# Engines report ahead of the score units, second keys on GpSimd, embedding projection in three bank pairs

## The reference

```python
def nsa_mixer(u, ...):                       # layer 1, 16 heads of 64 in 4 key groups
    q, kv, gates = split(u @ w_in)           # three branches: compressed, selected, window
    o = g0*softmax(q @ ck)@cv + g1*softmax(rope(q) @ ks)@vs + g2*softmax(rope(q) @ kw)@vw
    return o @ w_o

def channel_and_ple(h, p_i, g_pre, g_post, w_ff_in, w_ff_out, w_pg, w_pp):
    u = rmsnorm(h, g_pre)
    f = square(relu(u @ w_ff_in)) @ w_ff_out
    h = h + rmsnorm(f, g_post)
    return h + sigmoid(h @ w_pg) * (p_i @ w_pp)     # gate product, embedding projection
```

## Time and profile before

| | |
|---|---|
| median of 3 runs | 1681.08 us |
| the profiled execution's own time | 1680.83 us |
| its span, first to last instruction | 1677.9 us |
| busy: TensorE, weight load, VectorE, ScalarE, GpSimd | 1616.1, 1480.2, 824.3, 647.9, 109.2 us |
| granted TensorE clock, mean over the span | 0.987 |
| idle of TensorE ahead of L389 that ends with ACT L838 | 5.5 us in 6 waits |

### The profile page before, as it was taken

One profiled execution on the slowest core, in us unless ns is written; L12 is line 12 of the kernel. 1 busy time (PEld: TensorE's weight loads), 2 busy tenths in 40 slices (PEclk: granted clock), 3 DMA queues, 4 the chain that ended last, 5 costly groups with the idle time before them and its releaser, 6 DMA issues.

```text
span 1677.9 us, 32224 instructions
## 1 busy us (share of the span) xinstructions
PE 1616.1 (96%) x13788; PEld 1480.2 (88%) x13788; DVE 824.3 (49%) x1099; ACT 647.9 (39%) x1141; POOL 109.2 (7%) x138
## 2 busy tenths in 40 slices
PE   8999899999999999999999889999999999999998
PEld 7787799999999998999999555556999999999988
DVE  6988547444342436632342565652464433334462
ACT  5444654232231324522232456664442322323242
POOL 1000000000000000000240332210000000000000
PEclk9999999999999999999999879999999999999999
DMA  7533162323222222231246100002222222222211
GB/s 207 155 100 104 35 207 76 101 76 98 79 81 96 76 101 76 76 103 56 76 145 206 58 1 1 1 14 76 77 85 91 87 91 85 92 84 93 88 64 54
DMA packets 139623, 145.69 MB, mean 87 GB/s; under 512 B 6562, under 2 KB 131314, under 8 KB 139279
## 3 DMA queue, kind: packets, MB, share of 16 engines
q1 hardware_dynamic: 138207, 136.94, 25.9%
q0 software_dynamic: 1280, 6.75, 1.3%
HBM read 130.79 MB, written 10.87 MB: 84 GB/s over the span
## 4 chain that ended last, share of the span: by engine, by line
PE 87%; DVE 7%; ACT 4%; issue 1%; DMA 0%; SPq 0%; DVEq 0%; ACTq 0%
PE ps L389 63%; PE ps L522 2%; PE ps L1207 2%; PE ps L1056 2%; PE ps L1055 2%; PE ps L1057 2%; PE ps L1724 2%; PE ps L1704 1%; PE ps L1706 1%; DVE w_lo L374 1%; PE ps L1651 1%; PE ps L575 1%; PE ps L1649 1%; ACT w_hi L369 1%; DVE neg_max L1838 1%
## 5 line engine op out<-in xcount | busy, mean ns | idle before, releaser
L389 PE MATMUL ps<-x_hi,w_hi 128*128 128x272 f32 x1664 | 361.9, 291 | 15.0 <-ACT ple_proj L838 4.3
L389 PE MATMUL ps<-x_hi,w_lo 128*128 128x272 f32 x1664 | 358.2, 289 | 0.0
L389 PE MATMUL ps<-x_lo,w_hi 128*128 128x272 f32 x1664 | 357.5, 289 | 0.0
L374 DVE TENSOR_TENSOR w_lo<-w_raw,w_hi 128x2048 fp32r<-128x2048 f32 x101 | 233.8, 2315 | 141.4 <-ACT w_hi L369 139.5
L369 ACT ACTIVATE w_hi<-w_raw 128x2048 fp32r<-128x2048 f32 x101 | 192.6, 1907 | 267.9 <-PE ps L389 265.0
L389 PEld LDWEIGHTS ps<-x_hi,w_hi 128*128 128x128 f32 x1664 | 267.4, 189 | 24.5 <-issue 11.5
L389 PE MATMUL ps<-hid_hi,w_hi 128*128 128x272 f32 x1280 | 268.1, 289 | 2.2 <-DVE hid_lo L2028 1.5
L389 PEld LDWEIGHTS ps<-x_lo,w_hi 128*128 128x128 f32 x1664 | 267.9, 190 | 0.0
L389 PE MATMUL ps<-hid_hi,w_lo 128*128 128x272 f32 x1280 | 267.4, 288 | 0.0
L389 PE MATMUL ps<-hid_lo,w_hi 128*128 128x272 f32 x1280 | 266.6, 288 | 0.0
L389 PEld LDWEIGHTS ps<-x_hi,w_lo 128*128 128x128 f32 x1664 | 266.2, 189 | 0.0
(11 more groups left out here) (379 smaller groups left out, 2124.1 us busy)
## 6 DMA issues: line engine op xcount, KB each, us to landing
w_raw<-in_ffn_w_in SPq DMA_DIRECT2D x64, 512.0 KB, 4.5
w_raw<-in_ffn_w_out SPq DMA_DIRECT2D x64, 512.0 KB, 4.2
w_raw<-in_nsa_w_in SPq DMA_DIRECT2D x20, 512.0 KB, 4.5
w_raw<-in_ple_w_gate SPq DMA_DIRECT2D x16, 512.0 KB, 4.2
w_raw<-in_conv_w_in SPq DMA_DIRECT2D x15, 512.0 KB, 5.7
w_raw<-in_conv_w_out SPq DMA_DIRECT2D x8, 512.0 KB, 3.9
w_raw<-in_nsa_w_o SPq DMA_DIRECT2D x8, 512.0 KB, 4.4
conv_in_turned<-conv_in SPq DMA_DIRECT2D x16, 203.2 KB, 2.6
```

Source lines behind the costliest of these rows:

```text
L374: dve.tensor_tensor(WL[par][:, :], RAW[par][:, :], WH[par][:, :].bitcast(F32), ALU.subtract)\
L389: m = pe.matmul(o_, w[par][:, wcols:wcols + P], x[:, k, c_], start=f, stop=l)
```

## The change

It has three parts. (1) The embedding projection uses bank pairs 0, 1 and 3 in the order 0, 1, 3, 0, 1, 3, 0, 3; the copies of blocks 2, then 3 and 4 move ahead in ScalarE's list; the gate product's first slab waits for seven copies, not eight. (2) The three reports of `leave_phase` move into the sample part, ahead of the last early score units (TensorE: one, VectorE: three, ScalarE: two). The eight sample copies move from the end of the sample part to between lead units 5 and 6. Both shifts of the first pair and their rows stand ahead of the compressed branch of group 0 on VectorE; on TensorE the first shift stands behind unit 5 instead of unit 4, the second behind unit 7; `cmp_exp(0)` moves behind unit 8 on ScalarE. (3) GpSimd makes the third query set and the keys of group 1 right behind the second query set, ahead of the compressed blocks; a query set reports each half.

```diff
+        PLE_BLK = (0, 1, 3, 0, 1, 3, 0, 3)
+        PLE_FREE = (-1, 0, None, 1, 2, 3, 4, 6)
...
             for mb in range(NC):
-                pe_block(pe, s % 2, mb % 2, b + mb, s, mb, PH, PL, None, 0, nk=2, width=D)
+                if PLE_FREE[mb] is not None:
+                    pe.wait_ge(blk_free, b + PLE_FREE[mb])
+                pe_block(pe, s % 2, PLE_BLK[mb], b + mb, s, mb, PH, PL, None, 0, nk=2, width=D, free=False)
...
-            pe_slab_by_chunk(pe, s, b, XH, XL, x_ready, 8 * nx)
+            pe_slab_by_chunk(pe, s, b, XH, XL, x_ready, 8 * nx, free=1)
...
             ple(1)
+            ple(2)
             for c in range(NC):
-                if c + 2 < NC:
-                    ple(c + 2)
                 act.wait_ge(S["r_ready"], 8 * nr + c + 1)
                 L(act.activation(XH[:, c, :], R[:, c, :], ACT.Copy), S["xh_ready"], wait=False)
+                if c == 0:
+                    ple(3)
+                if c < 4:
+                    ple(c + 4)
...
             turn(3)
+            leave_phase(pe)
             unit(3)
...
             out_t(3)
+            leave_phase(act)
             unit(2)
             unit(3)
...
             turned(3)
+            leave_phase(dve)
             unit(1)
             unit(2)
             unit(3)
+
+        def sample_columns(dve, L):
             dve.wait_ge(S["ots_ready"], 4)
...
             def scores(i):
                 c, half, u = s_head(i)
-                if half == 0 and u == 0:
-                    pe.wait_ge(S["q_ready"], c + 1)
+                if u == 0:
+                    pe.wait_ge(S["q_ready"], 2 * c + half + 1)
...
             def rest():                                  # TensorE
-                for i in range(EARLY, LEAD):
-                    scores(i)
-                    if i == EARLY:
-                        pe.wait_ge(S["os_ready"], 4)
-                        pe.wait_ge(S["ots_ready"], 4)
-                        shifts(0, 0)
-                    if i == EARLY + 1:
-                        pe.wait_ge(S["cmp_blocks"], 2)
-                        cmp_scores(0, None)
-                    if i == EARLY + 2:
-                        shifts(1, 0)
+                pe.wait_ge(S["os_ready"], 4)
+                pe.wait_ge(S["ots_ready"], 4)
+                scores(EARLY)
+                scores(EARLY + 1)
+                shifts(0, 0)
+                scores(EARLY + 2)
+                pe.wait_ge(S["cmp_blocks"], 2)
+                cmp_scores(0, None)
+                scores(EARLY + 3)
+                shifts(1, 0)
                 steps()
...
                     if p + LEAD < N_S:                   # ScalarE
                         sums(p + LEAD)
+                    if p == 0:
+                        cmp_exp(0)
...
                 shift(0)                                 # VectorE
-                for i in range(EARLY, LEAD):
-                    maxima(i)
-                    if i == EARLY:
-                        rows(0)
-                    if i == EARLY + 1:
-                        cmp_shift(0)
-                        shift(1)
-                    if i == EARLY + 2:
-                        rows(1)
+                maxima(EARLY)
+                rows(0)
+                maxima(EARLY + 1)
+                sample_columns(dve, L)
+                maxima(EARLY + 2)
+                shift(1)
+                maxima(EARLY + 3)
+                rows(1)
+                cmp_shift(0)
...
-                    if p % 12 == 2 and p // 12 + 1 < KG:
+                    if p % 12 == 2 and 2 <= p // 12 + 1 < KG:
                         keys(p // 12 + 1)
...
             def rest():                                  # GpSimd
                 queries(1)
+                queries(2)
+                keys(1)
                 L(pool.memset(BDC[:, :, :, :], 0.0))
                 ...
-                for c in range(2, CK):
+                for c in range(3, CK):
                     queries(c)
```

More of the change, by code:

```diff
@@ L406, in pe_block, with pe_slab_by_chunk @@
             m.then_inc(blk_full, 1)
-        def pe_slab_by_chunk(pe, s, b, xh, xl, ready, x0, between=None):
-            pe.wait_ge(blk_free, b)
+        def pe_slab_by_chunk(pe, s, b, xh, xl, ready, x0, between=None, free=0):
+            pe.wait_ge(blk_free, b - free)
             pe.wait_ge(w_lo, s + 1)
@@ L485, in pe_two_slabs, with pe_linear @@
                 chunk(1, k, 1)
-        def pe_linear(pe, s0, b0, x0, xh=XH, xl=XL, between=None, then=None, last=None):
-            pe_slab_by_chunk(pe, s0, b0, xh, xl, x_ready, x0, between)
+        def pe_linear(pe, s0, b0, x0, xh=XH, xl=XL, between=None, then=None, last=None, free=0):
+            pe_slab_by_chunk(pe, s0, b0, xh, xl, x_ready, x0, between, free)
             if then:
@@ L756, in gate_pe @@
             if l == 0:
-                pe_linear(pe, s, b, 8 * nx)
+                pe_linear(pe, s, b, 8 * nx, free=1)
                 return
-            pe_slab_by_chunk(pe, s, b, XH, XL, x_ready, 8 * nx)
+            pe_slab_by_chunk(pe, s, b, XH, XL, x_ready, 8 * nx, free=1)
             for j in range(1, 4):
@@ L837, in ple @@
                 act.wait_ge(blk_full, b + m + 1)
-                act.activation(two(G[:, m, :]), blk(m % 2), ACT.Copy).then_inc(blk_free, 1)
+                act.activation(two(G[:, m, :]), blk(PLE_BLK[m]), ACT.Copy).then_inc(blk_free, 1)
             ple(0)
@@ L1791, in rest @@
                     sums(i)
-                    if i == EARLY + 2:
-                        cmp_exp(0)
                 for p in range(N_T):
@@ L1817, in keys @@
                 ka, kb = KA[g % 2], KB[g % 2]
[L1818 to L1824, removed]
+                dve.wait_ge(S["t_full"], 12 * (g - 1))
                 for br in range(2):
@@ L1891, in rest @@
             def rest():
-                L.count[S["k_ready"]] = 1
+                L.count[S["k_ready"]] = 2
                 shift(0)
-                for i in range(EARLY, LEAD):
-                    maxima(i)
-                    if i == EARLY:
-                        rows(0)
-                    if i == EARLY + 1:
-                        cmp_shift(0)
-                        shift(1)
-                    if i == EARLY + 2:
-                        rows(1)
+                maxima(EARLY)
[7 more added lines that the diff above has]
+                cmp_shift(0)
                 for p in range(N_T):
@@ L1939, in queries, with keys @@
                     L(pool.tensor_tensor(QA[c % 3][other, half, :], q, QA[c % 3][own, half, :].bitcast(F32), ALU.subtract),
-                      S["q_ready"] if half else None)
-            def first_keys():
+                      S["q_ready"])
+            def keys(g):
+                ka, kb = KA[g % 2], KB[g % 2]
+                if g >= 2:
+                    pool.wait_ge(S["t_full"], 12 * (g - 1))
+                else:
+                    for br in range(2):
+                        L(pool.tensor_scalar(kb[HD:P, br, :].rearrange("p (o n) -> p o n", n=P),
+                                             ONE[HD:P, :].rearrange("p (o n) -> p o n", o=1).broadcast_to([HD, QT, P]),
+                                             SELC[HD:P, br:br + 1], None, ALU.mult))
                 for br in range(2):
                     rows = slice(br * HD, (br + 1) * HD)
[L1946 to L1952, removed]
+                    L(pool.tensor_copy(ka[rows, br, :], KT[rows, g, :]))
+                    L(pool.tensor_copy(ka[(1 - br) * HD:(2 - br) * HD, br, :], KT[rows, g, :]), wait=False)
+                    L(pool.tensor_tensor(kb[0:HD, br, :], KT[rows, g, :], ka[rows, br, :].bitcast(F32), ALU.subtract),
+                      S["k_ready"] if br else None)
             def early():
@@ L1957, in early @@
                 queries(0)
-                first_keys()
+                keys(0)
                 L(pool.tensor_scalar(LGT[:, :, :], GT[:, 0:QT, :], 1e-19, None, ALU.max), S["log_gate"], wait=False)
@@ L1982, in nsa_pe @@
             samp_pe(pe, unit)
-            leave_phase(pe)
             rest()
@@ L1994, in nsa_act @@
             samp_act(act, L, unit)
-            leave_phase(act)
             rest()
@@ L2023, in nsa_dve @@
             samp_dve(dve, L, unit)
-            leave_phase(dve)
             rest()
```

## The result

The changed kernel took 1668.66 us, the median of five runs (1664.92 to 1670.88), against 1678.90 us for five runs of the kernel before: a ratio of 0.9944, 95% interval 0.9923 to 0.9964. Measured once more, it was 1664.97 against 1676.99 us, 0.9925 (0.9904 to 0.9946). The ratios in this text are the recorded ones; they are not exactly the quotients of the medians (here 0.9939 and 0.9928). The prediction was 1668.5 us, from a gain of 12.5 us. By the medians the change gained 10.2 and 12.0 us: the forecast was right in sign and size. That the first median is within 0.2 us of the forecast is in part luck, since five runs of the kernel before had a median 2.2 us under the 1681.08 us known when the forecast was made.

The account below looks back on a forecast made before the run. TensorE itself bounds the kernel (87% of the span), so only its waits and clock can give time back. 7.8 + 0 + 4.7 = 12.5 us off 1680.83 gives 1668.3, stated as 1668.5 us; range 1660 to 1677.

Parts of the forecast that it names:

- their room: Embedding projection, layer 0: each ScalarE copy would end 0.4 us or more before it is needed.
- what was named as late next: Gate product, layer 0: the second slab's weight split, ending at 666.65, would not move, so 3.2 us saved, not 3.5.
- the slow stretch of layer 1: Layer 1, gate product's first slab: about 1.4 us lost to slow clock; 4.6 us saved at full clock, otherwise 3.4.
- the forecast one: Ahead of step 0: GpSimd's earlier list holds some VectorE operations for a whole GpSimd instruction, so step 0 gains nothing.
- the rival's rule: Sample copies on VectorE: each is held for one GpSimd instruction, so eight copies take 7.3 us; chance 0.20.
- the second shift, for which I had added 0.9 us: VectorE ahead of step 0: the second shift was to take 0.9 us more beside GpSimd's running list.
- The 1.8 us that I added for the compressed shift: Steps 0 to 6: group 0's compressed shift before unit 8's maxima and `cmp_exp(0)` cost 0 to 3 us, taken as 1.8.
- the 4 us for the slow stretch: Steps 0 to 6: the stretch at clock 0.54 would go, saving 0 to 4.6 us, taken as 4.
- No collision: Ahead of step 0: copies slip between GpSimd's instructions, clock stays full, step 0 gains 2.8 us; total 1662.6 us; chance 0.20.
- the slower one: Between units 5 and 6: GpSimd holds VectorE until its list ends, step 0 11.7 us late; 1683.3 us; chance 0.04.
- the bank order gains nothing: Embedding projection: ScalarE's copies come late in the new places too; total 1676 us; chance 0.06.
- one copy per instruction with a lower clock: Ahead of step 0: copies take 7.3 us, step 0 3.5 us late, steps 0 to 6 save 1.4; 1675 us; chance 0.20.

Follow-up runs that it names:

- attention parts alone: Changed kernel with the old bank order of the embedding projection (two bank pairs, old order of copies): 1673.29 us, ratio 0.9971 to the kernel before.
- GpSimd parked: Changed kernel with GpSimd waiting for step 0's scores between its second and third query set, VectorE's order untouched: 1664.14 us, ratio 0.9920 to before.
- late copies: Changed kernel with the eight VectorE sample copies moved to step 9: 1661.96 us, ratio 0.9903 to before; measured again 1661.85 us, 0.9907.
- late copies and GpSimd parked: Changed kernel with the sample copies in step 9 and GpSimd waiting for step 0 before its third query set: 1657.75 us (0.9896), again 1663.47 us (0.9909).

## Why the prediction was right

**Part 1, forecast 7.8 us, measured 7.7 (5.0 to 10.4).** Step by step: the gate product in layer 0 was to start at 654.4; it started at 655.19 in a trace that ran 0.86 us late there, so 0.07 off. Its second slab was to start near 666.7 behind the split; with the same shift it came 0.1 us later. In layer 1 the slab came 0.1 us later than forecast, once the 9.33 us gained ahead of it are taken off. All copies kept their room (the last one that the gate product needs ended at 654.76, 0.43 us ahead of it), and what was named as late next was late next. The clock stayed at 1.00 in 1616 to 1620 us, as I took it. One part of the 7.8 us is less sure than I had it: 1.4 us of it is the slow stretch of layer 1 in the traced execution of before. The attention parts alone keep the old bank order, and there the same wait (2.17 us, until 1611.23) had a clock of 1.00 behind it, and the first slab took 12.30 us instead of 13.81.

**Part 2, step 0 forecast to gain nothing: it gained nothing, and in the profiled pair lost 1.1 us** against the last sample transpose (16.23 to 17.30). Other traces have 18.09 for the old order and 17.26 to 18.75 for the new one, at different clocks, so a loss of 1 us can't be told from their scatter. The mechanism was the forecast one, and parking GpSimd shows it. The term that was mis-sized is the eight copies: two for each GpSimd instruction, four instructions, 3.7 us, were taken. Eight copies stood beside six instructions, 5.31 us, between that and the 7.3 us of one copy each. One copy for each instruction, the rival's rule, is what the rows show, with two copies more that went through in 0.19 us. The first shift's cast took 1.15 us where the stretch of before that I carried over had 0.48, and the second shift, for which I had added 0.9 us, cost only some 0.3 (0.47 for one operation of 0.17).

The rule that I weighed, from the Trainium skill, "SBUF — State Buffer", section "Who interferes with whom", says that copies and casts can take the ports shared with GpSimd and that reductions never do. The runs agree: 190 ns a copy beside an idle GpSimd and up to 1140 beside a busy one, with reductions at 1.22 to 1.23 us in both.

**Part 3, forecast 4.7 us, 6.5 in the profiled pair.** The wait of 2.0 us went and the clock in 1000 to 1010 us is at 1.00, both as forecast. The 1.8 us that I added for the compressed shift beside GpSimd did not come: steps 0 to 6 took 24.65 us, and 31.2 - 2.5 - 4.0 is 24.7. But the 4 us for the slow stretch were read from one execution of before. Two other traces with the keys on VectorE took 28.76 and 28.34 us for these steps, so that the part is worth about 4 us there. Parts 2 and 3 together were forecast at 4.7 us; the attention parts alone measured 4.9 (2.0 to 7.7).

**The rivals.** No collision is out (5.31 us, not 1.7), and so is the slower one, since GpSimd released VectorE at each instruction's end and reductions ran through. That the bank order gains nothing is out too. The case of one copy per instruction with a lower clock came true in half: the copies went nearly one by one, but steps 4 to 6 kept a clock of 1.00. The slow stretch around step 0 isn't the new wait's doing: it stands in the kernel before, and with GpSimd parked, behind a wait of 1.83 us, the clock was 0.51 in 968.40 to 972.40.

So the sum, 12.5 us, lies a little above both differences of the medians, 10.2 and 12.0 us, with two terms that were off by 1 to 2 us in opposite directions in the profiled pair. That they cancel is luck.

## What to carry to other kernels

Starting an engine's list earlier also moves it on top of whatever used to run while it was parked: look for strings of short VectorE copies and casts under it, and put them where GpSimd is idle (here step 9: 1.73 us instead of 5.31). A bank order is worked out by giving each copy its time and each block its need: that sum was right to 0.1 us. Where single executions differ by several microseconds, test the parts alone and let their measured ratios make the sum; the profiled pair, 15.9 us, overstated this change by a third to a half, and a slow stretch in one trace isn't yet a cost of the kernel.

## What the runs showed of the hardware

The granted clock differs from execution to execution in the same code. Two windows of the kernel with GpSimd parked, against 0.70 and 0.79 in the same windows of the kernel before and 0.71 and 0.95 in the changed one:

```profile
930.00:940.00 10.00, 7.01 (x137) 4.99 (x138) 5.96 (x17) 4.00 (x12) 3.73 (x7) 1.00 0.24 73
940.00:950.00 10.00, 8.30 (x175) 5.07 (x177) 5.97 (x19) 4.35 (x17) 0.00 (x0) 1.00 0.11 36
```

TensorE was busy for 7.0 to 8.6 of each 10 us in all three. From the last matmul of L1064 (the key and value projection, ahead of the sample part) to the last sample transpose it is 103.8 us here and 106.2 in the changed kernel. The twelve traces fall into two groups: in six the stretch takes 102.7 to 104.3 us, with a clock of 1.00 from 20 to 10 us ahead of that transpose, and in six 106.2 to 107.2 us, with 0.84 to 0.92 there. The kernel with late copies is in both groups (104.3 and 106.9), and so is the one with late copies and GpSimd parked (103.1 and 107.0). So such a stretch moves an execution by 2 to 4 us whatever the edit. What decides whether it comes isn't shown by these runs.

VectorE's two-input operations on 128x8 tiles can be held as well: in the kernel with late copies and GpSimd parked (its first run) one took 1.20 us at 976.63, where such an operation takes 0.17 elsewhere, and GpSimd's subtraction ran from 976.53 to 977.79.
